# Where a one-chunk-late group of matmuls stands in the product order of a gated recurrence

## The reference

```python
def _gla_scan(q, k, log_f, v, s0):
    def step(s, xs):
        qc, kc, gc, vc = xs
        a = jnp.cumsum(gc, axis=2)
        diff = a[:, :, :, None, :] - a[:, :, None, :, :]
        decay = jnp.exp(jnp.where(causal[:, :, None], diff, -jnp.inf))
        scores = jnp.sum(qc[:, :, :, None, :] * kc[:, :, None, :, :] * decay, axis=-1)
        o = jnp.einsum('bhts,bhsv->bhtv', scores, vc) + jnp.einsum('bhtk,bhkv->bhtv', qc * jnp.exp(a), s)
        a_last = a[:, :, -1:, :]
        s_new = jnp.exp(a_last[:, :, 0, :, None]) * s + jnp.einsum('bhsk,bhsv->bhkv', kc * jnp.exp(a_last - a), vc)
        return s_new, o
```

## Time and profile before

| | |
|---|---|
| median of three runs | 3556.19 us |
| profiled execution, its own time | 3561.7 us |
| its span in the profile | 3559.9 us |
| PE busy | 3353.4 us, 94% |
| VectorE busy | 1073.3 us, 30% |
| ScalarE busy | 959.6 us, 27% |
| GpSimd busy | 223.8 us, 6% |
| recurrence of layer 0 | about 2070 to 2239 us of the span |
| recurrence of layer 1 | about 3071 to 3185 us |

### The profile page before, as it was taken

One profiled execution on the slowest core, in us unless ns is written; L12 is line 12 of the kernel. 1 busy time (PEld: TensorE's weight loads), 2 busy tenths in 40 slices (PEclk: granted clock), 3 DMA queues, 4 the chain that ended last, 5 costly groups with the idle time before them and its releaser, 6 DMA issues.

```text
span 3559.9 us, 44823 instructions
## 1 busy us (share of the span) xinstructions
PE 3353.4 (94%) x18622; PEld 1875.6 (53%) x18622; DVE 1073.3 (30%) x2457; ACT 959.6 (27%) x1966; POOL 223.8 (6%) x256
## 2 busy tenths in 40 slices
PE   8999999999999989998999989979998999997999
PEld 4554454754464454753755767543324755763333
DVE  2224551022224461022252446130002254453011
ACT  1344230111335130113232345031112234441110
POOL 0000000000000000000000055000100000440000
PEclk9999999999999999999999999989999999998999
DMA  4221172311221172312101000139993101013997
GB/s 157 90 77 54 65 290 74 121 42 65 71 78 48 65 290 72 123 57 90 42 25 37 23 2 31 54 142 361 363 341 157 48 30 48 1 55 146 366 409 308
DMA packets 120263, 437.60 MB, mean 123 GB/s; under 512 B 13168, under 2 KB 15344, under 8 KB 119424
## 3 DMA queue, kind: packets, MB, share of 16 engines
q1 hardware_dynamic: 113040, 407.45, 31.3%
q0 software_dynamic: 7024, 27.30, 2.3%
HBM read 422.08 MB, written 12.62 MB: 122 GB/s over the span
## 4 chain that ended last, share of the span: by engine, by line
PE 85%; DVE 5%; DMA 4%; ACT 3%; issue 1%; POOL 1%; SPq 0%; DVEq 0%; ACTq 0%; POOLq 0%
PE bank L1799 82%; DMA ring<-in_stream 3%; PE bank L1914 1%; DMA h_sb<-in_stream 1%; ACT work L2161 0%; PE bank L856 0%; DVE work L2319 0%; DVE work L2321 0%; DVE h_sb L2482 0%; DVE work L1579 0%; PE bank L1986 0%; DMA work<-tokens,slot_tok 0%; DVE h_sb L1532 0%; DMA work<-in_stream 0%; DVE small L1578 0%
## 5 line engine op out<-in xcount | busy, mean ns | idle before, releaser
L1799 PE MATMUL bank<-h_sb,ring 128*128 128x512 f32 (+2 forms) x3200 | 1252.0, 547 | 28.0 <-ACT h_sb L1087 10.1
L1799 PEld LDWEIGHTS bank<-h_sb,ring 128*128 128x128 f32 (+1 forms) x3200 | 591.6, 190 | 586.1 <-issue 542.1
L1799 PE MATMUL bank<-y_sb,ring 128*128 128x512 f32 (+1 forms) x1152 | 474.1, 573 | 9.9 <-DVEq L225 9.9
L1799 PEld LDWEIGHTS bank<-y_sb,ring 128*128 128x128 f32 x1152 | 219.1, 191 | 259.9 <-issue 245.1
L2121 ACT ACTIVATE work<-bank 128x512 f32<-128x512 f32 (+1 forms) x256 | 129.7, 516 | 767.7 <-PE bank L1799 662.9
L1799 PE MATMUL bank<-ring,h_sb 128*128 128x128 f32 (+2 forms) x2144 | 284.8, 311 | 1.4 <-ACT work L1250 0.7
L1799 PEld LDWEIGHTS bank<-ring,h_sb 128*128 128x128 f32 (+2 forms) x2144 | 232.2, 185 | 42.3 <-issue 39.2
L1799 PE MATMUL bank<-work 128*64 128x128 f32 (+7 forms) x1712 | 235.7, 350 | 14.2 <-ACT work L2161 4.2
L1799 PE MATMUL bank<-ring,work 128*64 128x512 f32 (+2 forms) x920 | 224.2, 560 | 3.5 <-DMA ring<-in_stream 3.5
L1799 PEld LDWEIGHTS bank<-work 128*64 128x64 f32 (+2 forms) x1712 | 142.9, 164 | 94.2 <-issue 64.7
L1799 PE MATMUL bank<-y_sb,work 128*64 128x128 f32 (+2 forms) x920 | 170.8, 438 | 1.3 <-DMA y_sb<-in_stream 0.8
(11 more groups left out here) (298 smaller groups left out, 3279.6 us busy)
## 6 DMA issues: line engine op xcount, KB each, us to landing
ring<-in_stream SPq DMA_DIRECT2D x578, 512.0 KB, 5.2
y_sb<-in_stream SPq DMA_DIRECT2D x110, 512.0 KB, 8.1
h_sb<-in_stream SPq DMA_DIRECT2D x40, 512.0 KB, 14.8
work<-in_stream SPq DMA_DIRECT2D x20, 512.0 KB, 15.3
work<-in_bias SPq DMA_DIRECT2D x2, 2688.0 KB, 9.9
tokens<-work POOLq DMA_DIRECT2D x10, 512.0 KB, 4.1
work<-forget POOLq DMA_DIRECT2D x2, 1536.0 KB, 7.0
x_sb<-in_xT SPq DMA_DIRECT2D x4, 512.0 KB, 6.6
```

Of the source, the lines that this page charges most:

```text
L1799: return nc.tensor.matmul(o, a, b, start=first, stop=last, skip_group_check=True)
```

## The change

`products` gets a parameter `half`: half 0 issues A, half 1 issues B and then T. O of the chunk before is issued between the halves, and S always behind them, in every chunk but the last.

```diff
-                def products(i, ci):
+                def products(i, ci, half):
 
                     c, last = FLOW[PASSES[i][1]][ci], ci == N_CH - 1
-                    for n in range(2, 8):
+                    for n in range(2 + 3 * half, 5 + 3 * half):
                         for hh in range(2):
...
+                    if half == 0:
+                        return None
                     if not last:
                         freed["product"] += 1
                     top_products(i, c)
...
-                        made = products(i, ci) if wanted(l, FLOW[PASSES[i][1]][ci]) else None
-                        if 0 < ci < N_CH - 1:
-                            state(i, ci)
+                        here = wanted(l, FLOW[PASSES[i][1]][ci])
+                        if here:
+                            products(i, ci, 0)
                         if before:
                             outputs(*before)
-                        if ci == 0:
+                        made = products(i, ci, 1) if here else None
+                        if ci < N_CH - 1:
                             state(i, ci)
-                            if i in (3, 5):
-                                head_sums()
+                        if ci == 0 and i in (3, 5):
+                            head_sums()
```

## The result

| | before | changed |
|---|---|---|
| median | 3554.77 us (4 runs, 3549.74 to 3561.05) | 3577.51 us (4 runs, 3574.95 to 3581.06) |
| profiled execution | 3561.7 us | 3581.06 us |
| its span | 3559.9 us | 3579.3 us |
| PE busy | 3353.4 us | 3367.4 us |

The ratio of changed to before is 1.0062, with a 95% interval of 1.0049 to 1.0075: 22.7 us slower. The direction was right, and the time lies in the range, but only by half a microsecond (its upper end is 3578), and the loss is twice the 11.2 us of the forecast.

A forecast was written before the change was run, and what follows sets the result against it. PE, 94% busy, sets the pace; in layer 0 a 17.2 us chain behind chunk 2's T sets each pass. Terms summed to 9.7 us, plus 1.5 for the clock: 11.2 slower, 3567.4 us from 3556.2; range from just below 3552 to 3578.

The forecast's parts named there:

- The rival on the other side: Waits of B and the like that O covers are all that counts: 3.9 us faster, 3552 us; chance 0.25.
- the rival in which the clock falls at more borders: Borders between passes, both layers: longer idling lowers PE's clock at more borders or for longer, 3575 to 3581 us; chance 0.17.
- Point 1: Layer 0, passes 0 to 4: T of chunk 2 and its chain come 1.39 us later, in pass 3 1.1; 5.6 + 1.1 us.
- Point 2: Both layers: T's banks are awaited, 0.7 us at `head_sums` twice (layer 0), 0.6 at each recurrence's end; 1.4 + 1.2 us.
- The signs named beforehand: Layer 0's borders: PE's waits and GpSimd's idle time before its run each grow by about 1.4 us.
- Point 3: Behind the head norm, pass 5 of both layers: O covers B's waits for late copies, 1.0 us each, 2.0 us gained.
- Point 4: Layer 1's borders: the last chunk's T comes 1.1 us later, the chain ends 0.6 later in passes 0, 1, 2, 4; 2.4 us.
- Point 5: Layer 0, entry to pass 5: longer idling makes the granted clock fall there too; taken at 1.5 us, up to 2.7.

The follow-up runs named there:

- the pair with early exponentials: Kernel before and changed kernel, both with ScalarE making the next pass's exponentials a chunk earlier: 3543.4 and 3553.74 us.
- all but the last: Changed kernel, except that in the last chunk of each pass O goes back behind T: 3574.93 us, 1.0063 of the kernel before.
- changed, again: The changed kernel measured once more without any edit: 3574.17 us, 1.0054 of the kernel before.
- before, early exponentials: Kernel before with only ScalarE's program altered, making the next pass's exponentials a chunk earlier: 3543.4 us, 0.9955 of the kernel before.

## Why the prediction was right and where it failed

**The mechanism held.** The chain from T over ScalarE's program order, GpSimd and VectorE sets the pass: it took 17.27 to 17.70 us in passes 1 and 2 of both kernels while T moved by up to 3.39 us, and both ways of easing it (exponentials earlier, T first) made the kernel before faster, by 16.1 and 9.6 us. The rival on the other side, that only the covered waits count, is refuted. It drew on the advice of the Trainium skill ("Perfetto Trace Analysis", section "Optimization Strategy") to find the gaps of the most contended engine and let what they wait for start sooner. Followed for the gaps in front of B alone, it led the wrong way here: these gaps did close, and T, which releases the longer ones, came later.

**That the number fell into the range owes something to luck.** 3577.51 us lies half a microsecond below its upper end, and the sum behind the forecast had half of the loss. It also lies in the 3575 to 3581 us of the rival in which the clock falls at more borders, and that is not what the profile shows: layer 1's passes 1 to 4 ran at 1.00, and pass 5 of layer 0 was entered at full clock. Such falls do come in other executions (below), so that rival cannot be called wrong for the median, but the pieces found do not need it.

**Point 1, T of chunk 2, was too small.** Said: 6.7 us for passes 0 to 4. They grew by 10.9: passes 1 to 4 by 11.1 (12.2 from start to T2, less 1.1 in the chain), pass 0 not at all. The 12.2 divide into 5.6 for O's time; 2.8 for the switches (0.70 a pass, as the pair with early exponentials shows); 0.9 for the two new waits of O on the accumulators; 0.7 for `head_sums` in pass 3, which point 2 had counted; and 2.0 for the lower clock. 0.2 is left. The signs named beforehand show the same: GpSimd's idle time before its run grew by 2.4 us a pass where 1.4 was said, while PE's waits at the borders grew by 0.7 each and not by 1.4, the rest being busy time. Point 1 also took T of chunk 2 for the only gate. T of chunk 3 had 0.6 us of slack, which no row of a wait showed except the 0.32 in pass 3; I had read that row and taken it for a discount.

**The sentence that failed** is in the first part: "The order of pieces inside such a chunk costs nothing as long as nobody waits for one of them." It costs 0.20 us where O stands between A and B, and 0.35 in chunk 1. In layer 0 about twenty of the 35 places lie ahead of T2 or in the last pass, six of them in chunk 1, 4.9 us; the others fall inside the chain. With layer 1's 18 places, 3.6 us, this is up to 8.5 us that the sum had at nothing. Nothing in the timeline before was missing for it: the 0.17 us pauses at a change of shape stand in its weight loads too. I looked for waits and did not read that row as a price.

**Point 2** (waits for T's banks) was right: 0.70 against 0.7 and 0.51 against 0.6. **Point 3** (covered waits) as well: chunk 3 behind the head norm in pass 5 went from 4.60 us between its T and that before to 3.85, where 4.80 would be without the cover; in layer 1, 0.66 of waiting remained, on O itself. **Point 4** (layer 1, 2.4 us) has the right sign and half of the size, 4.6 by the two profiles; the switches (15 places in five passes, 3.0 us) would fill the gap by themselves, and "all but the last" speaks against the cause that it named. The size itself is uncertain, since the second profile of the changed kernel has 4.8 us more in these passes.

**Point 5, the clock**, was said at 1.5 us, for a fall at one more border (pass 5). In the first profile it did not come: pass 5 is entered after 1.11 us as before, and its first row takes 0.94 us. In the second profile of the same kernel it did, after the same wait. PE's timeline of "changed, again", the first product of pass 5:

```profile
2221.39 1.65 PE L1802 MATMUL bank<-h_sb 64*128 64x128 f32 x12 [1.10 <-DVE ring L479]
```

From there to the end of the recurrence are 31.28 us, where the first profile has 28.57: 2.7 us, the full price that the prediction had put on such a fall. Ahead of T2 the low clock lasted longer in passes 2 to 4 (in pass 4, 6.6 us at the lower level where it was 2.9) and shorter in passes 0 and 1; the net is 0.3 us.

**What stays open.** The pieces found come to 10.9 (passes 0 to 4 of layer 0), 1.9 (its pass 5 with the end, 26.72 to 28.57 us from the first product to the last head sums), 4.6 (five passes of layer 1) and 0.3 (its last pass at full clock: 21.48 us against 21.20 in "before, early exponentials", whose last pass has the order of before): some 18 us of the 22.7 between medians (20.5 in the second measurement of the same kernel). The remaining 2 to 5 us are of the size by which one profile of a kernel differs from another; a single fall of the clock was 2.7. How often the clock falls in either kernel, and whether the change makes it fall more often, no run separates.

## What to carry to other kernels

Before a group of matmuls is moved, follow what each of the groups it passes releases on other engines, in those engines' program order, and list every gate and its slack, not only the one that is seen to be last: the second had 0.6 us. Price each new change of array shape between neighbours, even where nobody waits. Where two profiles of one program disagree, compare the stretches that ran at the same granted clock. And where an engine with little to do stands in order behind the bounding engine's output, moving its independent work ahead (here ScalarE's exponentials by a chunk, 16.1 us faster, 0.9955 [0.994, 0.997]) was worth more than closing gaps of the busy engine.

## What was unexpected of the hardware

- At a change of TensorE's array shape between groups of matmuls the weight loads paused for 0.03 to 0.17 us; one change more in a chunk came with 0.20 us, two more with 0.35 us, and all of it counts as busy time of PE.
- A chain of operations over three engines repeats to 0.01 us (17.27 and 17.27, 13.42 and 13.42 in two profiles of one program), while PE's stretch ahead of it took 11.96 and 13.13 us in the same two, at a granted clock of 0.86 and 0.77.
- After the same wait of 1.1 us in front of pass 5, one execution of the changed kernel went on at full clock and another at the lower level.
